# Expert weights in chunks of half a contraction for both experts of a pair

## The reference, cut to what matters

```python
D_MODEL, D_EXPERT, N_EXPERTS, TOP_K = 1024, 512, 32, 2      # 256 tokens
def expert_block(args):
    idx, e = args
    xb = x_pad[idx]
    hb = jax.nn.silu(xb @ w_gate[e]) * (xb @ w_up[e])
    return hb @ w_down[e]
...
y = zeros.at[tok_pad].add(contrib)      # contrib = y_blocks * router weight
...
gate = sigmoid(rmsnorm_2(h, norm_ple[i]) @ w_ple_gate[i] + b_ple_gate[i])
h = h + gate * (p[i] @ w_ple[i])
```

## Time and profile before

| | us |
|---|---|
| median of the runs | 1731.73 (1731.1 to 1732.87) |
| span of the profiled execution, first to last instruction | 1726.6 |
| what lies around the span, by the median | 5.1 |
| PE busy in the span | 1630.1 (94%) |
| DVE, ACT, POOL busy | 722.2, 506.4, 231.9 |
| DMA moved in all | 528.24 MB, mean 306 GB/s |
| MoE of layer 0, first product to last | 615.6 to 1067.1 |
| MoE of layer 1 | 1230.1 to 1681.5 |

### The profile page before, as it was taken

How to read it: one execution, slowest core, us unless ns; L and a number is a source line. 1 busy time by engine, 2 the same in 40 slices (tenths; PEclk the granted TensorE clock), 3 DMA queues, 4 the chain that set the end, 5 groups by cost and what they waited for, 6 DMA issues and landing times.

```text
span 1726.6 us, 25582 instructions
## 1 busy us (share of the span) xinstructions
PE 1630.1 (94%) x10590; PEld 1110.1 (64%) x10590; DVE 722.2 (42%) x1348; ACT 506.4 (29%) x778; POOL 231.9 (13%) x151
## 2 busy tenths in 40 slices
PE   5998998999999999999999998998999999999997
PEld 2787797999989955454545454988645454445446
DVE  2567624999247532221212124779312121212135
ACT  3444345444453221111111114485211110101125
POOL 0407322677410000000000000000000000000000
PEclk9999888999999999999999999999999999999998
DMA  9224343353545679999999999316999999999990
GB/s 404 112 97 169 149 156 150 147 195 126 192 167 228 257 327 429 427 429 428 428 429 428 428 428 400 146 50 243 398 421 426 428 429 428 429 428 428 427 404 25
DMA packets 37957, 528.24 MB, mean 306 GB/s; under 512 B 4208, under 2 KB 4336, under 8 KB 5104
## 3 DMA queue, kind: packets, MB, share of 16 engines
q1 hardware_dynamic: 37296, 525.22, 73.4%
q10 hardware_dynamic: 576, 1.78, 0.3%
HBM read 525.94 MB, written 1.05 MB: 305 GB/s over the span
## 4 chain that ended last, share of the span: by engine, by line
PE 70%; DMA 16%; DVE 8%; ACT 3%; issue 1%; POOL 1%; SPq 0%; DVEq 0%; ACTq 0%; POOLq 0%
PE bank L534 22%; PE bank L1065 19%; PE bank L1095 9%; DMA ring<-in_w_up 9%; PE bank L1010 5%; DMA work<-in_w_up 4%; DMA ring<-in_dense 3%; PE bank L527 2%; DVE ring_rounded L1820 2%; PE bank L1031 1%; PE bank L1032 1%; PE bank L606 1%; ACT ring_rounded L1251 1%; PE bank L712 1%; PE bank L632 1%
## 5 line engine op out<-in xcount | busy, mean ns | idle before, releaser
L534 PE MATMUL bank<-work_rounded,ring_rounded 128*128 128x256 f32 (+1 forms) x2192 | 352.6, 292 | 10.8 <-DVE xn_rounded L1810 7.9
L1065 PE MATMUL bank<-ring,work 128*64 128x512 f32 x1536 | 337.4, 593 | 17.6 <-DMA ring<-in_w_up 15.3
L534 PEld LDWEIGHTS bank<-work_rounded,ring_rounded 128*128 128x128 f32 x2192 | 305.4, 191 | 20.6 <-issue 10.5
L534 PE MATMUL bank<-xn_rounded,ring_rounded 128*128 128x256 f32 (+1 forms) x1536 | 273.1, 290 | 4.2 <-DVE xn_rounded L1804 3.4
L1065 PEld LDWEIGHTS bank<-ring,work 128*64 128x64 f32 x1536 | 113.5, 137 | 233.7 <-issue 220.8
L534 PEld LDWEIGHTS bank<-xn_rounded,ring_rounded 128*128 128x128 f32 x1536 | 221.2, 194 | 8.7 <-issue 4.5
L2318 DVE TENSOR_TENSOR work<-work,bank 128x512 f32<-128x512 f32 x32 | 22.0, 688 | 420.2 <-PE bank L1065 420.2
L1707 POOL TENSOR_TENSOR ring_rounded<-ring,ring_rounded 128x2048 fp32r<-128x2048 f32 (+1 forms) x37 | 159.7, 4340 | 207.0 <-ACT ring_rounded L1251 207.0
L1773 POOL TENSOR_TENSOR work<-work_rounded,work 128x128 f32<-128x128 f32 x64 | 24.2, 399 | 1130.3 <-PE bank L1088 822.7
L1095 PE MATMUL bank<-ring,work 128*64 128x512 f32 x768 | 170.1, 595 | 0.0
L1251 ACT ACTIVATE ring_rounded<-ring 128x2048 fp32r<-128x2048 f32 (+1 forms) x84 | 147.7, 1803 | 54.5 <-PE bank L534 26.8
(11 more groups left out here) (333 smaller groups left out, 1696.1 us busy)
## 6 DMA issues: line engine op xcount, KB each, us to landing
ring<-in_dense SPq DMA_DIRECT2D x48, 2048.0 KB, 8.5
ring<-in_w_gate SPq DMA_DIRECT2D x48, 2048.0 KB, 22.5
ring<-in_w_up SPq DMA_DIRECT2D x48, 2048.0 KB, 25.5
ring<-in_w_down SPq DMA_DIRECT2D x48, 2048.0 KB, 27.0
work<-in_w_gate SPq DMA_DIRECT2D x16, 2048.0 KB, 23.2
work<-in_w_up SPq DMA_DIRECT2D x16, 2048.0 KB, 25.6
work<-in_w_down SPq DMA_DIRECT2D x16, 2048.0 KB, 27.0
ring<-in_dense SPq DMA_DIRECT2D x8, 1408.0 KB, 6.3
```

The lines of the kernel that those rows point to most:

```text
L534: last = mm(out, rv(high_store[r][:, at:at + P]), rv(x[part][k]), start=opens and k == 0 and j == 0, stop=closes and k == n_k - 1 and j == 2)
L1065: ins = mm(b[64 * y:64 * y + 64, :], xg[:, k, 64 * y:64 * y + 64], ws[y][:, 512 * k:512 * k + 512], start=k == 0, stop=k == KT - 1)
```

## The change

Each chunk now holds half of the contraction (4 of 8 row groups for gate and up, 2 of 4 for down) for both experts of the pair. PE waits for a chunk before the products that read it and signals after them, and SP loads a slot when its own half has been read. A chunk of 2 MiB is now, per partition, two pieces of 8 KiB from two experts instead of one of 16 KiB from one. In down, the order of products is half of the contraction outermost, so that result half 0 is complete after three quarters of the products instead of after one half; `down_mm` counts 3 per pair. In the last pair, the scatter of pair 14 stands ahead of the up products, and DVE's `add` of it ahead of the multiplication with up.

```diff
-            def into_slots(place, w, pair):
-                for y in range(2):
-                    sp.dma_start(slots[place][y], w[pair * 2 + y]).then_inc(S[names[place][y]], 16)
+            def into_slot(out, full, w, pair, part):
+                sp.dma_start(out.rearrange("p (y c) -> p y c", y=2), w[pair][:, :, CHUNK // 2 * part:CHUNK // 2 * part + CHUNK // 2]) \
+                    .then_inc(S[full], 16)
 
             def load_pair(pair, place):
-
-                sp.wait_ge(S["down_mm"], pair * 2 + 2 * (done - 1))
-                into_slots(place % 4, gate, pair)
+                for part in range(2):
+                    sp.wait_ge(S["down_mm"], pair * 3 + (3 * (done - 1) - 2 + 2 * part))
+                    into_slot(slots[place % 4][part], names[place % 4][part], gate, pair, part)
                 load_rest(pair, place)
 
             def load_rest(pair, place):
-                sp.wait_ge(S["gate_mm"], pair + done)
-                into_slots((place + 1) % 4, up, pair)
-                sp.wait_ge(S["up_mm"], pair + done)
-                into_slots((place + 2) % 4, down, pair)
+                for part in range(2):
+                    sp.wait_ge(S["gate_mm"], pair * 2 + (2 * done - 1 + part))
+                    into_slot(slots[(place + 1) % 4][part], names[(place + 1) % 4][part], up, pair, part)
+                for part in range(2):
+                    sp.wait_ge(S["up_mm"], pair * 2 + (2 * done - 1 + part))
+                    into_slot(slots[(place + 2) % 4][part], names[(place + 2) % 4][part], down, pair, part)
...
-                    ws = weights(h, x, kind)
-                    for k in range(KT):
-                        for y in range(2):
-                            ins = mm(b[64 * y:64 * y + 64, :], xg[:, k, 64 * y:64 * y + 64],
-                                     ws[y][:, 512 * k:512 * k + 512], start=k == 0, stop=k == KT - 1)
-                    ins.then_inc(S[sem], 1)
-
-                pe.wait_ge(S["scat_add"], i * 4 + layer * (4 * PAIRS + 5) + 1)
-                if last:
-                    scatter(i + 1)
-                else:
+                    if kind and last:
+                        scatter(i + 1)
+                    for part in range(2):
+                        ws = weights(h, x, kind, part)
+                        for k in range(4):
+                            for y in range(2):
+                                ins = mm(b[64 * y:64 * y + 64, :], xg[:, 4 * part + k, 64 * y:64 * y + 64],
+                                         ws[:, y, 512 * k:512 * k + 512], start=part + k == 0, stop=part * k == 3)
+                        ins.then_inc(S[sem], 1)
+
+                if not last:
+                    pe.wait_ge(S["scat_add"], i * 4 + layer * (4 * PAIRS + 5) + 1)
                     gather(i + 1)
...
-                ws = weights(h, x, 2)
-                for half in range(2):
-                    for j in range(4):
-                        for y in range(2):
-                            at = D * j + 512 * half
-                            ins = mm(bank[6 + half][64 * y:64 * y + 64, :], hidT[:, j, 64 * y:64 * y + 64],
-                                     ws[y][:, at:at + 512], start=j == 0, stop=j == 3)
-                    ins.then_inc(S["down_mm"], 1)
+                for part in range(2):
+                    ws = weights(h, x, 2, part)
+                    for half in range(2):
+                        for j in range(2):
+                            for y in range(2):
+                                at = D * j + 512 * half
+                                ins = mm(bank[6 + half][64 * y:64 * y + 64, :], hidT[:, 2 * part + j, 64 * y:64 * y + 64],
+                                         ws[:, y, at:at + 512], start=part + j == 0, stop=part * j == 1)
+                        if part or half:
+                            ins.then_inc(S["down_mm"], 1)
...
+                else:
+                    add(i)
                 dve.wait_ge(S["sg_sb"], i + done + 1)
...
-                add(i)
+                    add(i)
```

More of the change, by code:

```diff
@@ L134, in plan @@
         last = layer * PAIRS + PAIRS
-        for c, reader in enumerate((("down_mm", 2 * last - 2), ("gate_mm", last), ("up_mm", last))):
-            for y in range(2):
-                free[first[f"moe{layer}"] + 2 * c + y] = reader
+        for c, reader in enumerate((("down_mm", 3 * last - 3), ("gate_mm", 2 * last), ("up_mm", 2 * last))):
+            for part in range(2):
+                free[first[f"moe{layer}"] + 2 * c + part] = (reader[0], reader[1] - (1 - part if c else 0))
     slot, arrival, load_after, splits, high_slot, high_after = {}, {}, {}, [], {}, {}
@@ L143, in plan @@
                   (first["w_up"], 1): ("vn_mm", 8), (first["w_up"] + 1, 2): ("o_mm", 4),
-                  (first["w_out"] + 1, LOAD_SLOTS): ("vn_mm", 8), (first["w_in_b"], RING): ("down_mm", 2 * PAIRS)}
+                  (first["w_out"] + 1, LOAD_SLOTS): ("vn_mm", 8), (first["w_in_b"], RING): ("down_mm", 3 * PAIRS)}
     for name, count, _ in DENSE:
@@ L439, in _ @@
             layer = int(name[3:])
-            gate, up = (t[w][layer].rearrange("e (p j) f -> e p (j f)", j=KT) for w in ("w_gate", "w_up"))
-            down = t["w_down"][layer].rearrange("e (p j) f -> e p (j f)", j=4)
+            gate, up = (t[w][layer].rearrange("(i y) (p j) f -> i p y (j f)", y=2, j=KT) for w in ("w_gate", "w_up"))
+            down = t["w_down"][layer].rearrange("(i y) (p j) f -> i p y (j f)", y=2, j=4)
             done = layer * PAIRS
@@ L468, in _ @@
             for c in early:
-                load(base + c, (gate, up, down)[c // 2][c % 2], CHUNK)
+                load_first(c)
             load_embedding()
             sp.wait_ge(*((S["h_ready"], 2 * KT), (S["lru_h"], KT))[layer])
-            sp.dma_start(odd[0], gate[2]).then_inc(S["odd_full0"], 16)
+            into_slot(odd[0], "odd_full0", gate, 1, 0)
             for c in order[len(early):]:
-                load(base + c, (gate, up, down)[c // 2][c % 2], CHUNK)
-            sp.dma_start(odd[1], gate[3]).then_inc(S["odd_full1"], 16)
+                load_first(c)
+            into_slot(odd[1], "odd_full1", gate, 1, 1)
             load_rest(1, 3)
@@ L1033, in scatter, with weights @@
                     last.then_inc(S["scat_mm"], 1)
-            def weights(h, x, kind):
+            def weights(h, x, kind, part):
                 turn, place = divmod(3 * x + kind, 4)
                 if place == 3:
-                    for y in range(2):
-                        pe.wait_ge(S[f"odd_full{y}"], h * 48 + 16 * (layer * TURNS + turn + 1))
-                    return odd
-                for c in (2 * place, 2 * place + 1):
+                    pe.wait_ge(S[f"odd_full{part}"], h * 48 + 16 * (layer * TURNS + turn + 1))
+                    w = odd[part]
+                else:
+                    c = 2 * place + part
                     pe.wait_ge(S[f"slot_full{c}"], h * 48 + 16 * turn + ARRIVAL[FIRST[f"moe{layer}"] + c])
-                return ring[2 * place:2 * place + 2]
+                    w = ring[c][:]
+                return w.rearrange("p (y c) -> p y c", y=2)
             pe.wait_ge(S["tok_sb"], 4 * (layer + 1))
@@ L1556, in experts @@
             def experts(i, last=False, product=None):
-                act.wait_ge(S["gate_mm"], i + done + 1)
+                act.wait_ge(S["gate_mm"], i * 2 + 2 * done + 2)
                 act.activation(sg, bank[0][:], ACT.Silu).then_inc(S["sg_sb"], 1)
@@ L1571, in experts @@
                         split_half()
-                    act.wait_ge(S["down_mm"], i * 2 + 2 * done + half + 1)
+                    act.wait_ge(S["down_mm"], i * 3 + 3 * done + half + 2)
                     act.activation(rv(y_high[half]), bank[6 + half][:], ACT.Identity, scale=slot_w).then_inc(S["y_high"], 1)
@@ L2315, in experts @@
                     select(i + 1)
+                else:
+                    add(i)
                 dve.wait_ge(S["sg_sb"], i + done + 1)
-                dve.wait_ge(S["up_mm"], i + done + 1)
+                dve.wait_ge(S["up_mm"], i * 2 + 2 * done + 2)
                 v.tensor_tensor(hh, sg, bank[1][:], ALU.mult).then_inc(S["hh_sb"], 1)
```

4 lines of the change are left out of this document (3 added, 1 removed).

## The result

The changed kernel takes 1740.41 us (median of 8 runs), the kernel before 1731.78 in the same rounds: ratio 1.0047, 95% interval 1.0034 to 1.0060, so 0.47% slower, 8.1 us by the ratio and 8.6 by the medians. The forecast was 1735.5, range 1725 to 1742. The profiled span went from 1726.6 to 1736.5, 9.9 us. In the runs that have both, device time is 1.6 to 1.9 us above this span. By that the profiled execution of the kernel before took some 1728.4 us (an estimate), 3.3 under its median, and that of the changed kernel, 1738.31, 2.1 under its own; so 3.3 of the 5.1 us that I took for what lies around the span was that execution being a short one.

What follows compares the result with a forecast made beforehand. The DMA stream was taken to end each MoE stage, PE just ahead. Earlier start and smaller pieces: -3.45 + 5.2 in layer 0, -3.2 + 5.2 in layer 1, together +3.8 us on 1731.73: 1735.5 us, range 1725 to 1742.

Steps and rivals of the forecast that it cites:

- What sets the end of a stage: Both MoE stages: each ends when the DMA stream ends, plus 7.9 us of ACT and DVE; PE 0.7 us ahead.
- single waits: PE in the MoE stages: most 1.9 us stalls go, some 7 us lead a layer, costed at nothing beyond the stream.
- Earlier start: Start of each stage's stream: first load issued after half of gate, -3.45 us in layer 0, -3.2 in layer 1.
- Smaller pieces: Expert chunks in the full queue: 8 KiB pieces 1.2% slower, 0.059 us a chunk, +5.2 us a layer.
- Rival B: Expert stream: pieces 2 MiB apart cost more, or the 2.3% bound holds; +13.2 us, 1744.9 us; chance 0.10.
- Sum: Both layers, start plus pieces: +1.75 us in layer 0, +2.0 in layer 1, together +3.8 us.
- Rival C, the clock: Behind each stage: PE idles longer, its clock falls sooner; up to 1.5 us a layer, +3, 1738.5 us; chance 0.12.
- The order inside down, the scatter: Last pair: result half 0 1.8 us later, scatter net 1 to 2 us of PE time; both hidden by the stream.

Runs made afterwards that it cites:

- joint waits: Changed kernel, but PE waits for both chunks of a kind ahead of its first product, release staying single; 1742.20 us, ratio 1.0061.
- whole rows: Changed kernel, but each chunk is loaded as whole 16 KiB rows of one expert (wrong data for the products); 1726.95 us, ratio 0.9964.
- pieces of one expert: Changed kernel, but each chunk comes from one expert in 8 KiB pieces, a partition's two lying 1 MiB apart (wrong data); 1740.73 us, ratio 1.0041.
- the filled kernels: Unread products put in PE's gaps at each stage's end: 6 a layer in the kernel before, 1727.22 us; 12 in the changed kernel, 1733.18 us.
- joint release: Changed kernel, but SP reloads both slots only when the whole kind has been multiplied, PE still waiting singly; 1745.63 us, ratio 1.0078.

## Why the prediction came out as it did

*What sets the end of a stage.* Right. In the changed kernel ACT stands for the ple load for 5.5 us where it stood for 0.7, so PE's lead grew by 4.8 us, and neither single waits (joint waits: stages within 1.7 and 0.9 us of the changed kernel, in opposite directions) nor the scatter's place (two kernels) move the load's landing by more. Looking only at PE's 94% and its 23.2 us of waits would have promised a gain.

*Earlier start.* Right in kind, and in size for layer 0 (3.1 by whole rows against before, 3.45 forecast). In layer 1 whole rows gain 1.8 where I took 3.2. I had added up two idle stretches there, 2.4 and 0.8 us, as if the earlier issue closed both; 3.2 was a most that it could give, and I took it as the value.

*Smaller pieces.* With the start of layer 1 this is the term that was mis-sized. I took 1.2%, 5.2 us a layer, from windows of 4 and 5 us. The long windows give 428 against 421, which is 1.6%, 0.08 us a chunk and 7.2 us a layer; whole rows against pieces measures 6.3 and 5.7 us in the stages. I had compared with the one short window of 16 KiB rows at 426 instead of the 400 us at 428, and averaged over windows that spread by 8 GB/s. The 1.6% against the long one was in the text, as the worse reading. As a rate it was the right one; in the stages the pieces cost 6.0 us a layer on average, between the 5.2 and the 7.2. Rival B's bound of 2.3% was too high, and its reason, the distance of the two pieces, is refuted by the pieces of one expert. Of the two rules from the Trainium skill's page "DMA: Bandwidth & Descriptors", full rate from 512 B (section Specifications) would give 0, and 3 cycles a packet (section "Why small descriptors are slow (HBM only)") an estimated 2.5 us a layer; the runs show more than either.

*Sum.* Forecast +3.8, measured +8.1 (8.6 by the medians). The stages give 7.1 of it where I had 1.75 + 2.0. Of the 3.35 between, the pieces are 1.1 + 0.5 (6.3 and 5.7 for twice 5.2), and the start 0.35 + 1.4.

*Rival C, the clock.* It was not in the sum. The stretch at the lower level did get longer, as that rival had it (10.2 us against 3.4), but what it adds to the difference is not settled: 0.7 or 2.6 us by the filled kernels, with nothing and the 3 that I gave it both inside the intervals. The stages alone give 7.1 of the 8.1. What I had not seen is that the kernel before pays for the lower level as well, 5.4 us.

*The order inside down, the scatter.* Costed at nothing, since the stream hides them; right for the change. The cover I named for down's order is real: with joint waits it is gone and the price is 2.1 and 2.3 us, against 1.8 forecast. So "nothing beyond the stream" held for single waits and this order together, not for each alone.

*Not settled.* How long the lower level lasts in the executions of each kernel, and so whether the clock has a part in the difference: profiles of several executions of one kernel would tell, and none were taken. Nor why joint release costs more with small pieces (4.6, 3.7) than the start gains with whole rows (3.1, 1.8).

## What to carry to other kernels

Ask which stream ends last before paying for finer waits: here PE got 5 us further ahead and the DMA behind it ended the stage. A finer chunk pays at the start of a stage, where the queue follows the releases, and costs in the full queue by the size of its pieces; so cut fine where the queue is empty and whole where it is full, and keep to single releases until it is full: one pair of them gave nothing, three gave 0.24%. Price a rate from the longest window that the trace has.

## What was not expected of the hardware

- Halving the contiguous piece from 16 to 8 KiB costs 1.6% of the rate of a full queue (428 to 421 GB/s), whether the two pieces of a row lie in one expert or in two.
- With twice the pieces in the queue, SP's issue of one load, 0.37 us in the median for ring loads of gate and up and 0.47 for those of down, takes up to 8.7 us. The instructions of one line in the changed kernel (x: min/median/max in ns, first and last start):

```profile
L447 SPq DMA_DIRECT2D ring<-in_w_down x48: 367/470/8689, 581.6 to 1618.9; - x48
```

and the same line in the kernel before:

```profile
L448 SPq DMA_DIRECT2D ring<-in_w_down x44: 328/348/1154, 629.5 to 1612.4; - x44
```

  With whole rows and all else as in the changed kernel, the same line takes at most 0.51 us. The queue stayed full while SP stood (421 GB/s), so it cost nothing here. Whether it would where SP has other work was not tried.
- 6 to 12 products a layer that nobody reads, put in gaps of 1.0 to 2.6 us behind a stage, took 5.4 and 7.2 us off the kernel before and the changed one, with the granted clock behind the stage at its upper level, 1.00, instead of 0.57 and 0.50.
